# An input projection with the weights held still, changed to one with the activations held still

## The reference, cut to what matters

```
h = rmsnorm(x) ; u = h @ w_in                      # 5664 columns
q, k, v, f, xs, B, C, z, dt = split(u)             # 1024 1024 1024 16 1024 256 256 1024 16
y_fox = forgetting attention(q, k, v, f)           # 16 heads of 64
xs, B, C = silu(causal_dwconv4(xs, B, C))
y_ssd = rmsnorm(ssd_scan(xs, B, C, dt) * silu(z))  # 16 heads of 64, state 128
x = x + concat(y_fox, y_ssd) @ w_out
x = x + (silu(causal_dwconv3(g)) * up) @ w_down    # g, up = rmsnorm(x) @ w_gate_up, 5632 each
x = x + sigmoid(rmsnorm(x) @ w_ple_gate) * (p @ w_ple_proj)
out = rmsnorm(x)
```

## Time and profile before

| | |
|---|---|
| median of 3 runs | 1210.88 us (1210.5 to 1211.56) |
| the profiled execution's own time | 1210.68 us |
| its span, first to last instruction | 1208.6 us |
| TensorE busy | 1196.4 us (99%), granted clock 0.997 |
| VectorE busy | 807.8 us (67%) |
| ScalarE busy | 669.6 us (55%) |
| DMA | 263.13 MB, mean 218 GB/s |

### The profile page before, as it was taken

How to read it: one execution, slowest core, us unless ns; L and a number is a source line. 1 busy time by engine, 2 the same in 40 slices (tenths; PEclk the granted TensorE clock), 3 DMA queues, 4 the chain that set the end, 5 groups by cost and what they waited for, 6 DMA issues and landing times.

```text
span 1208.6 us, 17282 instructions
## 1 busy us (share of the span) xinstructions
PE 1196.4 (99%) x5752; PEld 1002.9 (83%) x5752; DVE 807.8 (67%) x1188; ACT 669.6 (55%) x898; POOL 48.1 (4%) x69
## 2 busy tenths in 40 slices
PE   9999999999999999999999999999999999999996
PEld 8888888888888788888888888888888888888885
DVE  5698787788866576666766767667655555545554
ACT  6465787775555555555645655555444444445554
POOL 3200220002100000000000000000000000000000
PEclk9999999999999999999999999999999999999998
DMA  9566886445688878778787787887767676767653
GB/s 284 171 181 185 239 243 186 122 124 174 217 233 269 244 229 248 246 238 248 227 244 245 240 246 230 246 250 230 239 214 214 207 214 213 212 206 257 198 191 105
DMA packets 225496, 263.13 MB, mean 218 GB/s; under 512 B 13840, under 2 KB 168548, under 8 KB 225316
## 3 DMA queue, kind: packets, MB, share of 16 engines
q1 hardware_dynamic: 223588, 257.39, 69.9%
q0 software_dynamic: 1824, 5.04, 1.4%
q10 hardware_dynamic: 32, 0.01, 0.0%
HBM read 242.94 MB, written 17.87 MB: 216 GB/s over the span
## 4 chain that ended last, share of the span: by engine, by line
PE 97%; DMA 1%; ACT 1%; DVE 1%; issue 0%; SPq 0%; ACTq 0%; DVEq 0%
PE ps L1052 13%; PE ps L1054 13%; PE ps L1053 13%; PE ps L392 10%; PE ps L1088 7%; PE ps L1087 7%; PE ps L1089 7%; PE ps L463 6%; PE ps L465 6%; PE ps L464 6%; PE ps L390 5%; PE ps L366 2%; PE ps L982 1%; PE ps L997 0%; PE ps L962 0%; PE ps L949 0%
## 5 line engine op out<-in xcount | busy, mean ns | idle before, releaser
L355 DVE TENSOR_TENSOR w_lo<-w_raw,w_hi 128x1024 fp32r<-128x1024 f32 x412 | 506.2, 1233 | 335.3 <-ACT w_hi L350 334.0
L350 ACT ACTIVATE w_hi<-w_raw 128x1024 fp32r<-128x1024 f32 x412 | 434.6, 1058 | 419.1 <-PE ps L1054 205.6
L1052 PE MATMUL ps<-w_hi,h_parts 128*128 128x512 f32 x704 | 274.0, 389 | 0.7 <-DVE h_parts L1445 0.7
L1054 PE MATMUL ps<-w_hi,h_parts 128*128 128x512 f32 x704 | 273.9, 389 | 0.0
L1053 PE MATMUL ps<-w_lo,h_parts 128*128 128x512 f32 x704 | 273.9, 389 | 0.0
L392 PE MATMUL ps<-h_parts,w_hi 128*128 128x512 f32 x512 | 180.1, 394 | 0.0
L1052 PEld LDWEIGHTS ps<-w_hi,h_parts 128*128 128x128 f32 x704 | 132.1, 188 | 28.5 <-DVE h_parts L1445 1.1
L1054 PEld LDWEIGHTS ps<-w_hi,h_parts 128*128 128x128 f32 x704 | 132.1, 188 | 27.5
L1053 PEld LDWEIGHTS ps<-w_lo,h_parts 128*128 128x128 f32 x704 | 132.1, 188 | 27.4
L390 PE MATMUL ps<-h_parts,w_lo 128*128 128x256 f32 x512 | 145.7, 285 | 0.0
L1087 PE MATMUL ps<-w_hi,act_parts 128*128 128x512 f32 x352 | 136.9, 389 | 0.0
(11 more groups left out here) (257 smaller groups left out, 1159.0 us busy)
## 6 DMA issues: line engine op xcount, KB each, us to landing
w_raw<-in_w_gate_up SPq DMA_DIRECT2D x352, 256.0 KB, 3.5
w_raw<-in_w_down SPq DMA_DIRECT2D x88, 512.0 KB, 4.8
w_raw<-in_w_in SPq DMA_DIRECT2D x87, 512.0 KB, 4.2
w_raw<-in_w_out SPq DMA_DIRECT2D x32, 512.0 KB, 4.8
w_raw<-in_w_ple_gate SPq DMA_DIRECT2D x32, 512.0 KB, 4.7
unit_cols<-unit_dram SPq DMA_DIRECT2D x88, 128.0 KB, 3.0
unit_dram<-rms SPq DMA_DIRECT2D x22, 256.0 KB, 3.1
unit_dram<-unit_spare SPq DMA_DIRECT2D x22, 256.0 KB, 3.5
```

The costliest lines, as they stand in the source:

```text
L350: act.activation(parts(n)[0], w_raw[:, n % RING, :], ACT.Copy).then_inc(w_hi_made, 1)
L355: dve.tensor_tensor(lo, w_raw[:, n % RING, :], hi, ALU.subtract).then_inc(w_lo_made, 1)
L1052: pe.matmul(dst, a, hi, start=first and kk == 0, stop=False)
L1054: mm = pe.matmul(dst, b, hi, start=False, stop=last and kk == 1)
```

## The change

All eleven groups of the input projection are now by token. B/C, x, q, k and z are left by ScalarE with the reciprocal RMS as a scale for each token (`leave_group`; for q it is multiplied by 1/8 beforehand), VectorE transposes the 32x32 blocks, SyncE writes the tile to DRAM and reads it back turned. `spread_rms`, the joining of partial sums and the ferries of the GpSimd queue go. The order becomes B/C, x0, x1, k0, q0, k1, q1, v0, v1, z0, z1; the first group, by pass, is now B/C. q comes back in runs of 32 floats (16 loads for a group), the others in runs of 128 floats (4 loads). The convolution works in blocks of 32 tokens: for each half group three passes of 4 operations (2 long, 2 of 7 to 21 values for a partition that reach over a block's edge). `turn_xs` moves from 7 to 13 chunks behind the end of its x group (now chunks 28 and 36, were 30 and 38), `gate_norm` from 6 to 11 behind z1. The output projection's halves run o0 to o3, o0 to o3, in place of o0 to o2, o0 to o2, o3.

```diff
-                in_groups.append(Group(n + "ab"[i], win_v, c + i * HALF, "h", banks(), KP // 2, cols=HALF))
+    in_groups = [Group(n, win_v, c, "h", (SET_A, SET_B)[i % 2], KP) for i, (n, c) in enumerate(in_cols)]
-    halves = [(g, 0, KP // 2) for g in range(3)] + [(g, KP // 2, KP) for g in range(3)] + [(3, 0, KP)]
+    halves = [(g, a, a + KP // 2) for a in (0, KP // 2) for g in range(D // COLS)]
...
+        GROUP_OUT, GROUP_BACK, GROUP_READY = LEAD + 5, LEAD + 6, LEAD + 6
...
+        def group_to_dram(sp, name):
+
+            i = turned_names.index(name)
+            for t, blocks in enumerate((first_blocks[:, :], group_spare(i))):
+                sp.wait_ge(group_turned, TT * i + t + 1)
+                if t == 0 and i > 0:
+                    sp.wait_ge(*group_landings(turned_names[i - 1]))
+                sp.dma_start(group_dram[t], blocks).then_inc(group_out, 16)
...
+        def group_from_dram(sp, name):
+
+            i = turned_names.index(name)
+            sp.wait_ge(group_out, 16 * TT * (i + 1))
+            if name in conv_names and i > 0:
+                sp.wait_ge(conv_step, 2 * CONV_STEPS * i)
+            if name[0] == "z":
+
+                sp.wait_ge(mix_lo_made, WT // 4 * (int(name[1]) + 1))
...
+            def leave_group(g):
+
+                i = turned_names.index(g.name)
                 act.wait_ge(w_used, done[g.name] + 1)
...
+                scale = rms_q_col if g.name[0] == "q" else rms_col
+                for t in range(TT):
+                    copy(unit_tok[:, t, :], ps[:, g.banks[t], :], scale[:, t:t + 1]).then_inc(group_left, 1)
...
-            all_after(end["x0"] + 7, "turn_xs", 0)
-            all_after(end["x1"] + 7, "turn_xs", 1)
-
-            b0 = end["x1"] + 9
+            all_after(e0 + 14, "cb", 0)
+            all_after(e0 + 16, "cb", 1)
+            all_after(end["x0"] + 13, "turn_xs", 0)
+            all_after(end["x1"] + 13, "turn_xs", 1)
+
+            b0 = end["x1"] + 17
...
-            all_after(end["z1"] + 6, "gate_norm")
+            all_after(end["z1"] + 11, "gate_norm")
```

More of the change, by code:

```diff
@@ L39 @@
 MT = COLS // P
-HALF = COLS // 2
-CONV_STEPS = 7
+BLK = 32
+CONV_STEPS = 12
 GATE_STEPS = 10
@@ L174, in build @@
         ROWS_AHEAD = 4
[L175 to L178, removed]
+        NB = P // BLK
+        blocked = lambda name, offset: at(name, [P, 2, TT * NB, MT, BLK], offset=offset)
+        qE, qO = (at(n, [P, WT, T], offset=a * K1) for n, a in (("qE", 0), ("qO", 56)))
+        kE, kO = (blocked(n, a * K1) for n, a in (("kE", 8), ("kO", 16)))
         probT_hi, probT_lo = (at(f"probT_{n}", [P, 2, 3 * P], F32R, offset=(24 + 3 * i) * K1) for i, n in enumerate(("hi", "lo")))
@@ L379, in multiply_by_pass @@
             pe.wait_ge(*lo_made)
[L380 to L398, removed]
+            return one_pass(w_lo, hHi)
         UNIT_BANKS = (SET_C, SET_A)
@@ L521, in all_after @@
                 after(dve_after, n + LEAD, name, *args)
[L523 removed]
+            all_after(e0 + 1, "turn_p")
             for g in in_groups:
[L525 to L536, removed]
[L537 to L539 removed]
@@ L549, in plan @@
-            all_after(end["q0"] + 10, "cums")
-            after(dve_after, end["q0"] + 11 + LEAD, "make_row", 0)
-            after(dve_after, end["q0"] + 12 + LEAD, "make_row", 1)
-            all_after(end["bc"] + 10, "cb", 0)
-            all_after(end["bc"] + 13, "cb", 1)
-            all_after(end["x0"] + 7, "turn_xs", 0)
-            all_after(end["x1"] + 7, "turn_xs", 1)
-            b0 = end["x1"] + 9
+                n = end[g.name]
+                step = "leave_v" if g.name[0] == "v" else "leave_group"
@@ new lines, in plan @@
+                after(act_after, n + LEAD, step, g)
+                after(dve_after, n + LEAD, step, g)
+                if g.name[0] != "v":
+                    after(sp_before, n + GROUP_OUT, "group_to_dram", g.name)
+                    if g.name[0] == "q":
+                        for b in range(2):
+                            after(sp_before, n + GROUP_BACK + 2 * b, "queries_from_dram", g.name, (2 * b, 2 * b + 1))
+                    else:
+                        after(sp_before, n + GROUP_BACK, "group_from_dram", g.name)
@@ new lines, in plan @@
+                if g.name in conv_names:
+                    for b in range(2):
+                        u = 2 * conv_names.index(g.name) + b
+                        m = n + GROUP_READY + b * KC - b
+                        after(act_after, m, "conv_first", u)
+                        for back in range(1, KC):
+                            after(dve_after, m + back - 1, "conv_taps", u, back)
+                        after(act_after, m + KC - 1, "conv_silu", u)
+            all_after(e0 + 1, "turn_par")
@@ new lines, in plan @@
+            after(pe_after, e0 + 2, "fd")
+            after(dve_after, e0 + 2 + LEAD, "fd")
+            after(act_after, e0 + 5 + LEAD, "fd")
+            after(pe_after, e0 + 4, "turn_fd")
+            after(dve_after, e0 + 4 + LEAD, "logits")
+            after(dve_after, e0 + 6 + LEAD, "softplus")
+            after(pe_after, e0 + 8, "turn_falls")
+            after(dve_after, e0 + 8 + LEAD, "cumulate")
+            all_after(e0 + 10, "cums")
+            after(dve_after, e0 + 11 + LEAD, "make_row", 0)
```

344 lines of the change are left out of this document (146 added, 198 removed).

## The result

The changed kernel takes 1218.4 us (median of 4 runs, 1218.17 to 1220.69); the kernel before, run beside it, 1210.69 (1210.42 to 1211.56). The ratio is 1.0062, 95% interval 1.0049 to 1.0074: 0.6% slower, where 0.3% faster was forecast, and above the range. The profiled span grew from 1208.6 to 1216.3.

What follows compares the result with a forecast made beforehand. TensorE, busy 99% of the span, was taken to bound the kernel; 2.5 + 0.9 + 0.45 = 3.9 us off 1208.6 gave a span of 1204.7, plus 2.3 a time of 1207.0 us, range 1204.8 to 1212.5.

Steps and rivals of the forecast that it cites:

- the change part by part: The prediction's pricing of each part of the change, summed to 3.9 us off the 1208.6 us span.
- the way by DRAM: Input projection groups written out and loaded back turned: 10.4 us against 13.6 us of cover, so hidden by TensorE's chunks.
- `gate_norm`: Norm behind z1: GpSimd's sum of squares ready with 0.7 us of margin, bounds a stall of 0 to 1.5 us.
- order of the output halves: Output projection's new order of halves: same columns, so zero cost, bounds -0.5 to +1 us.
- TensorE's sum: Input projection: 2.5 us from by-token groups, 0.9 from the first group, 0.45 from `spread_rms`, together 3.9 us off.
- Rival D: Input projection: by-token orientation gives nothing, only `spread_rms` and part of the first group; 1210 us, chance 0.06.
- VectorE held: VectorE's load: some 10 us less in all, and about 1 us ahead of `cums`.
- B: VectorE comes late at `cums`, `turn_xs` and `gate_norm`, 3 us lost: 1210 us, chance 0.17.
- The hold at chunk 88: Weight load queued behind z0's load back lands 6 to 7 us late; chunk 88's low part has about 2 us to spare.
- C: SyncE's queue holds weight loads at chunks 24, 32 and 88 until TensorE waits, 7 us lost: 1214 us, chance 0.17.
- the cost taken, zero: q's 16 loads in short runs: at most about 7 us of shared queue, cost zero, bound 1 us.
- A: Likeliest case, all is hidden across the kernel: 1207.0 us, bounds 1205.3 to 1209, chance 0.60.

Runs made afterwards that it cites:

- a_line: The changed kernel with its two small tiles made one, so hand-placed tiles start 64 bytes lower: 1211.8 us, ratio 1.0004; again (a_line_2) 1209.79 us, 0.9995.
- a_line_z: a_line with z0's load back and z0's SiLU and gating three chunks later: 1206.87 us, ratio 0.9964; again 1207.1 us, 0.9966.
- z_only: The changed kernel with z0's load back and z0's SiLU and gating three chunks later, hand-placed tiles left where they were: 1216.19 us, ratio 1.0048.
- b_plus64: The kernel before with all hand-placed tiles 64 bytes later, nothing of the change in it: 1221.52 us, ratio 1.0086.
- b_plus32: The kernel before with all hand-placed tiles 32 bytes later, nothing of the change in it: 1221.26 us, ratio 1.0084.
- a_line_g: a_line with only z0's SiLU and gating three chunks later, its load back left in place: 1208.98 us, ratio 0.9984.
- a_line_b: a_line with only z0's load back three chunks later on SyncE's queue, its SiLU and gating left in place: 1208.86 us, ratio 0.9986.

## Why the prediction was wrong

**The step that failed** is in the change part by part: it priced the input projection, VectorE, the way by DRAM and `gate_norm`, and gave *order of the output halves* "Zero, bounds -0.5 to +1" on the ground of the same columns. The output projection and the down stage were thereby counted at an unchanged pitch. They have 1440 matmuls at 0.0067 us more, 9.5 us that no bound held and no rival named; undone, they give back 0.6 to 0.8% (a_line, a_line_z against z_only), and put into the kernel before they cost it 0.86% (b_plus64). The missing term is in the diff all the same: one small tile more moves everything placed behind it. The condition that the prediction named for being wrong, a pitch by token other than 0.2275, has happened, but by the operands' places, not by what runs beside.

**TensorE's sum held.** 3.9 us off were reckoned; 4.0 are measured at the last transposes of attention and 4.7 at the end of the input projection, 0.8 more than the sum: 2.72 a chunk in the first group and in x0 (2.73 taken), 3.10 beside the scan. Rival D falls: the orientation gives its part.

**VectorE held**: 9.6 us less for some 10. No wait of TensorE at `cums` or `turn_xs`. The scan that feeds `cums` ends at 66.59 and `cums` starts at 66.77: in time, but with 0.2 us and not the 1 us reckoned. There B was rightly called unlikely.

**The way by DRAM held at x0 and x1, not at z0.** At chunks 24 and 32 ScalarE waited 4.2 and 1.8 us for held weights, and TensorE for nothing. The hold at chunk 88 was seen and given "about 2 us to spare" for its own low part. That one came in time; those of the next three chunks did not, 1.2 us lost in the changed kernel and 0.9 to 1.6 without the misplacement. Nor was the next thing behind them followed: the later SyncE's queue, the later z1's load back, its gating and GpSimd. *`gate_norm`* was given 0.7 us of margin with a stall of 0 to 1.5; by the starts it lost 1.2 in the changed kernel and 1.7 to 2.1 without the misplacement. Both terms were priced as if independent, and the first feeds the second. So B's place and C's mechanism are one chain; by a_line against a_line_z it costs 0.35%, 4 us, nearer to B's 3 than to C's 7. The Trainium skill's page DMA: Bandwidth & Descriptors warned of runs under 512 B; q's loads of 32 KB landed in 3.1 to 3.9 us, as long as k's of 128 KB (3.3 to 4.0), a quarter of the bytes in the same time, which does not speak against the page, though no run here tells short runs from small loads. No engine waited for them, and the cost taken, zero, held.

**The sum, corrected**: -4.7 to the end of the input projection; +5.0 in the output projection (2.5 placement, 1.2 low parts, 1.2 `gate_norm`); +7.0 in the down stage from its first to its last matmul, placement again; +0.4 elsewhere: 7.7, the difference of the spans. With both faults taken out a_line_z gives 1206.9 and 1207.1, where the forecast said 1207.0. That bears out its terms, not its number: the change as it stands takes 1218.4.

Two slips of the working change nothing in this. A's lower end by its own terms is 1205.6, not 1205.3 (1210.9 - 5.3). And if B and D lie within 0.2% and half of C does, slower has 0.09 and not 0.16.

Open: why b_plus64 and b_plus32 lose 0.85% where 1440 x 0.0067 is 0.79%. They were already 1.0 us late at the last transposes of attention (274.35 against 273.33). Two traces of one program differ by 0.8 there (a_line and a_line_2), so this may be no effect of placement; z_only is not late there. Open too is the wait for h's last tiles at the beginning of gate/up, 0.5 to 1.6 us in most traces and 2.4 in a_line_g.

## What to carry to other kernels

Read a diff for tiles as well as for instructions: where large tiles are placed behind small ones, a tile of 8 bytes can move them all, so pin the start, and keep held and streamed operands as far apart as in a version whose pitch you have measured. Here alike within 128 bytes was fast wherever it was measured, but all those pairs were alike within 256 too. Compare the pitch of a stage that the diff doesn't touch: where it moved at an equal clock and with no wait, test placement first. When a queue is held, don't stop at the item behind the wait: follow it to the next items of the same queue, here the weights of the next three chunks, and to the one whose consumer has the least margin, here z1 and its GpSimd sum eleven chunks on. Measure what TensorE lost between the starts of its matmuls, since the named waits showed 1.3 us of 2.4. And undo two faults together as well as singly, for a slower engine can hide part of the waits that the other fault makes.

## What the runs showed of the hardware

- A matmul of 512 columns in fp32r, held and streamed operands at the same place within 128 bytes of a partition: 0.2267 us apart; 32 or 64 bytes different: 0.2333, 2.9% more, at a granted clock of 1.00 in both, and with the weight loads at 188 ns in both. Both operands 64 off: 389 ns long as with none. A difference of 128 was not run. Held at 0 and streamed at 64 (h_parts with last_hi and last_lo, after) the three forms read 397, 390 and 392 where before they read 394, 389 and 389, a smaller loss; streamed at 32 (b_plus32) all three read 395. What in the chip makes it was not tried.
- After TensorE stood 2.2 us (a_line_b, 318.9 to 321.1) its granted clock was 0.50 for some 3.3 us, which cost 1.6 us; after 1.9 us (a_line) it stayed at 1.00.
- GpSimd's squares and sums of one half took 9.5 us (313.02 to 322.54), with VectorE's low parts beside them.
